# Attention scores of a two-block transformer: the heads of a unit taken in turns from both halves of the partitions

## What is computed

```
# first block, once in each of two layers: 2 key heads, each for 4 query heads
s = jnp.einsum('bnqhgd,bnkhd->bhgnqk', qb, kb)
s = jnp.where(mask, s, MASK_VALUE)
m = jnp.maximum(jnp.max(s, axis=-1, keepdims=True), sink)
p = jnp.exp(s - m)
p = p / (jnp.sum(p, axis=-1, keepdims=True) + jnp.exp(sink - m))
o = jnp.einsum('bhgnqk,bnkhd->bnqhgd', p, vb)
# second block: 8 heads, a bias of accumulated forget gates
logits = jnp.einsum('bhqd,bhkd->bhqk', qb, kh).astype(jnp.float32) * scale
logits = logits + (cqb[..., :, None] - c[..., None, :])
probs = jax.nn.softmax(logits, axis=-1)
```

## Time and profile before

| | |
|---|---|
| median of three runs | 824.11 us (824.04 to 824.52) |
| the profiled execution, its own time | 824.92 us |
| its span, first to last instruction | 823.2 us |
| TensorE matmuls | busy 808.2 us (98%) |
| weight loads | busy 730.8 us (89%) |
| VectorE | busy 597.8 us (73%) |
| ScalarE | busy 476.4 us (58%) |
| mean from memory | 182 GB/s |

### The profile page before, as it was taken

The page is one execution under the profiler, slowest core; times in us unless marked ns, Lnnn a source line. Parts: engine busy times, 40 slices in busy tenths (PEclk is TensorE's granted clock), DMA queues, the critical chain, the costliest instruction groups (busy, mean ns, idle before and its releaser), DMA issues.

```text
span 823.2 us, 12834 instructions
## 1 busy us (share of the span) xinstructions
PE 808.2 (98%) x5184; PEld 730.8 (89%) x5184; DVE 597.8 (73%) x690; ACT 476.4 (58%) x562; POOL 28.8 (3%) x63
## 2 busy tenths in 40 slices
PE   8999999999999999999999999999999999999998
PEld 8988899998998889999887999999887888888877
DVE  6799765768588787576667557556879878787793
ACT  6875775433676585543457634433368656565682
POOL 8100000000000000210000000000000000000000
PEclk9999999999999999999999999999999999999999
DMA  7545343355435633256736434455119979797921
GB/s 260 187 160 187 132 147 108 134 198 181 148 113 200 205 103 104 103 178 187 242 103 205 154 103 154 154 172 187 52 52 364 332 261 342 265 330 266 345 102 52
DMA packets 70043, 149.65 MB, mean 182 GB/s; under 512 B 8458, under 2 KB 11104, under 8 KB 69984
## 3 DMA queue, kind: packets, MB, share of 16 engines
q1 hardware_dynamic: 69568, 148.78, 52.6%
q0 software_dynamic: 384, 0.04, 0.1%
q10 hardware_dynamic: 32, 0.01, 0.0%
HBM read 147.76 MB, written 1.05 MB: 181 GB/s over the span
## 4 chain that ended last, share of the span: by engine, by line
PE 87%; DVE 8%; ACT 3%; issue 1%; DMA 1%; SPq 0%; POOL 0%; DVEq 0%; POOLq 0%; ACTq 0%
PE mm L611 11%; PE mm L613 11%; PE mm L612 11%; PE mm L595 9%; PE mm L597 9%; PE mm L596 9%; PE aux L1072 4%; PE aux L1070 4%; PE aux L1071 4%; DVE sb_w_lo L1629 3%; PE aux L703 3%; PE aux L795 3%; PE aux L736 2%; PE aux L758 1%; DVE sb_gb L1629 1%
## 5 line engine op out<-in xcount | busy, mean ns | idle before, releaser
L1629 DVE TENSOR_TENSOR sb_w_lo<-sb_raw,sb_w_hi 128x2048 fp32r<-128x2048 f32 (+2 forms) x153 | 318.7, 2095 | 58.1 <-ACT sb_w_hi L1478 26.8
L1184 ACT ACTIVATE sb_w_hi<-sb_raw 128x2048 fp32r<-128x2048 f32 (+1 forms) x83 | 155.0, 1870 | 153.9 <-PE mm L613 115.7
L611 PE MATMUL mm<-sb_hT_hi,sb_w_hi 128*128 128x256 f32 x592 | 170.0, 287 | 0.0
L613 PE MATMUL mm<-sb_hT_hi,sb_w_lo 128*128 128x256 f32 x592 | 167.4, 283 | 0.0
L612 PE MATMUL mm<-sb_hT_lo,sb_w_hi 128*128 128x256 f32 x592 | 167.4, 283 | 0.0
L1478 ACT ACTIVATE sb_w_hi<-sb_raw 128x2048 fp32r<-128x2048 f32 x50 | 95.7, 1916 | 37.2 <-PE aux L1072 18.6
L595 PE MATMUL mm<-sb_w_hi,sb_hT_hi 128*128 128x512 f32 (+1 forms) x296 | 112.1, 379 | 4.1 <-DVE sb_w_lo L1629 4.1
L611 PEld LDWEIGHTS mm<-sb_hT_hi,sb_w_hi 128*128 128x128 f32 x592 | 113.4, 192 | 1.4 <-issue 1.3
L612 PEld LDWEIGHTS mm<-sb_hT_lo,sb_w_hi 128*128 128x128 f32 x592 | 113.5, 192 | 0.0
L613 PEld LDWEIGHTS mm<-sb_hT_hi,sb_w_lo 128*128 128x128 f32 x592 | 113.4, 192 | 0.0
L597 PE MATMUL mm<-sb_w_hi,sb_hT_lo 128*128 128x512 f32 (+1 forms) x296 | 110.3, 373 | 0.0
(11 more groups left out here) (400 smaller groups left out, 1364.4 us busy)
## 6 DMA issues: line engine op xcount, KB each, us to landing
sb_raw<-in_w_in SPq DMA_DIRECT2D x120, 512.0 KB, 4.5
sb_raw<-in_w_down SPq DMA_DIRECT2D x32, 512.0 KB, 5.7
sb_raw<-in_w_gate SPq DMA_DIRECT2D x31, 512.0 KB, 4.8
sb_raw<-in_w_up SPq DMA_DIRECT2D x31, 512.0 KB, 6.2
sb_raw<-in_w_out SPq DMA_DIRECT2D x16, 512.0 KB, 4.4
sb_raw<-in_w_up_attn SPq DMA_DIRECT2D x8, 512.0 KB, 4.4
sb_raw<-in_w_up_hgrn SPq DMA_DIRECT2D x8, 512.0 KB, 4.4
sb_raw<-in_w_o SPq DMA_DIRECT2D x8, 512.0 KB, 4.4
```

Source lines behind the costliest of these rows:

```text
L611: pe.matmul(dst, w[0][:, k, cs], acts[0][:, k, :], start=start, stop=False, skip_group_check=True)
L613: return pe.matmul(dst, w[1][:, k, cs], acts[0][:, k, :], start=False, stop=stop, skip_group_check=True)
L1184: act.activation(w_hi[:, slot(t), 0:width], raw[:, slot(t), 0:width], ACT.Copy).then_inc(hi_split, 1)
L1629: return dve.tensor_tensor(out_, a, b, op)
```

## The change

`score_unit` takes the heads in turns: the j-th of the lower half of the partitions, then the j-th of the upper half. Where there is a bias, both heads' score products come first, then both biases. Units 1 and 2 now hold two heads of each half: unit 1 heads 0, 1, 4, 5 and unit 2 heads 2, 3, 6, 7. The columns of a unit are filled in the order of its list of heads, so the lower half's heads write the first bank of `aux`, the upper half's the second. Unit 0 keeps its heads and columns. VectorE's steps read and write the sinks, the gate and `a_tok` for the two heads of each half as two pieces; `pv` takes the values of the new heads. No instruction is added or taken away.

```
--- before.py
+++ after.py
@@ -90,6 +90,11 @@
 WINDOWS = [(0, 1), (0,), (1,), (1,)]
 LAST_PIECES = [(0, 0, W), (1, 0, W // 2), (1, W // 2, W)]
 OUT_PIECES = [(tt, 0, W) for tt in range(TT)] + [(tt, W + a, W + b) for tt, a, b in LAST_PIECES]
+
+
+def unit_heads(u):
+
+    return list(range(8)) if u == 0 else [4 * g + 2 * (u - 1) + i for g in range(2) for i in range(2)]
 
 
 def slot(t):
@@ -728,17 +733,20 @@
             def score_unit(turn, u, qpart, kpart, bias2):
 
                 ps = begin(turn)
-                heads = range(8) if u == 0 else range(4 * (u - 1), 4 * u)
+                heads = unit_heads(u)
+                n = len(heads) // 2
                 keys = P if u == 0 else 2 * P
-                for i, h in enumerate(heads):
-                    dst = ps[:, i * keys:(i + 1) * keys]
-                    qtt = 0 if u == 0 else 1
-                    last = pe.matmul(dst, qpart(h, qtt), kpart(h, keys), start=True, stop=not bias2)
+                qtt = 0 if u == 0 else 1
+                for j in range(n):
+
+                    for i in (j, n + j):
+                        last = pe.matmul(ps[:, i * keys:(i + 1) * keys], qpart(heads[i], qtt), kpart(heads[i], keys),
+                                         start=True, stop=not bias2)
                     if bias2:
-
-
-                        r = slice(64 * (h // 4), 64 * (h // 4) + 64)
-                        last = pe.matmul(dst, selneg[r, h * P:(h + 1) * P], cT[r, 0:keys], start=False, stop=True)
+                        for i in (j, n + j):
+                            r, h = slice(64 * (i // n), 64 * (i // n) + 64), heads[i]
+                            last = pe.matmul(ps[:, i * keys:(i + 1) * keys], selneg[r, h * P:(h + 1) * P], cT[r, 0:keys],
+                                             start=False, stop=True)
                 end(turn, last)
 
             def p_transposes(turn, u, n):
@@ -756,7 +764,7 @@
                     for i in range(4):
                         for kt in range(2):
                             last = pe.matmul(ps[:, i * 64:i * 64 + 64], pT[:, (2 * i + kt) * P:(2 * i + kt + 1) * P],
-                                             vpart(4 * (u - 1) + i, kt), start=kt == 0, stop=kt == 1)
+                                             vpart(unit_heads(u)[i], kt), start=kt == 0, stop=kt == 1)
                 end(turn, last)
 
 
@@ -1742,6 +1750,15 @@
                 m = amask[:, 2:4, :] if block2 else amask[:, 0:2, :]
                 return m.rearrange("p a b -> p (a b)").unsqueeze(1).broadcast_to([P, 4, 256])
 
+            def paired(t):
+                return t.rearrange("p (g n) -> p g n", g=2)
+
+            def heads_in(u, t):
+
+                t = paired(t)
+                n = t.shape[2] // 4
+                return t if u == 0 else t[:, :, 2 * n * (u - 1):2 * n * u]
+
             def softmax_in(u, n, turn, sinks):
 
                 nh = 8 if u == 0 else 4
@@ -1757,11 +1774,11 @@
                 release(ins, aux_free[pair], value)
                 link(dve.tensor_reduce(ast[:, 0, a:a + nh], dst, AX, ALU.max))
                 if sinks is not None:
-                    hs = sinks[:, 0:8] if u == 0 else sinks[:, 4 * (u - 1):4 * u]
-                    link(tt_(ast[:, 0, a:a + nh], ast[:, 0, a:a + nh], hs, ALU.max))
+                    hs = heads_in(u, sinks)
+                    link(tt_(paired(ast[:, 0, a:a + nh]), paired(ast[:, 0, a:a + nh]), hs, ALU.max))
                 link(ts_(ast[:, 1, a:a + nh], ast[:, 0, a:a + nh], -1.0, ALU.mult))
                 if sinks is not None:
-                    link(tt_(ast[:, 3, a:a + nh], hs, ast[:, 1, a:a + nh], ALU.add))
+                    link(tt_(paired(ast[:, 3, a:a + nh]), hs, paired(ast[:, 1, a:a + nh]), ALU.add))
                     dve.sem_inc(S["sinkexp_in"], 1)
                 dve.sem_inc(S["S_ready"], 1)
 
@@ -1769,7 +1786,6 @@
 
                 nh = 8 if u == 0 else 4
                 a = a_at(u)
-                h0 = 0 if u == 0 else 4 * (u - 1)
                 tt = 0 if u == 0 else 1
                 dve.wait_ge(S["p_ready"], n * 3 + (u + 1))
                 if sinks is not None:
@@ -1778,13 +1794,13 @@
                 link(dve.reciprocal(ast[:, 0, a:a + nh], ast[:, 2, a:a + nh]))
                 pair, value = turn
                 dve.wait_ge(aux_ready[pair], value)
-                dst = a_tok[:, tt, h0 * 64:(h0 + nh) * 64]
-                ins = tt_(dst.rearrange("p (h d) -> p h d", h=nh),
-                          aux[pair][:, 0:nh * 64].rearrange("p (h d) -> p h d", h=nh),
-                          ast[:, 0, a:a + nh].unsqueeze(2).broadcast_to([P, nh, 64]), ALU.mult)
+                dst = heads_in(u, a_tok[:, tt, :])
+                ins = tt_(dst.rearrange("p g (h d) -> p g h d", d=64),
+                          aux[pair][:, 0:nh * 64].rearrange("p (g h d) -> p g h d", g=2, d=64),
+                          paired(ast[:, 0, a:a + nh]).unsqueeze(3).broadcast_to([P, 2, nh // 2, 64]), ALU.mult)
                 release(ins, aux_free[pair], value)
                 if gate is not None:
-                    link(tt_(dst, dst, gate[:, tt, h0 * 64:(h0 + nh) * 64], ALU.mult))
+                    link(tt_(dst, dst, heads_in(u, gate[:, tt, :]), ALU.mult))
                 if u == 2:
                     dve.sem_inc(S["a_ready"], 1)
 
```

## The result

The changed kernel takes 814.70 us, median of four runs (814.28 to 815.63), against 824.32 us for the kernel before, timed again beside it (824.04 to 825.24). The ratio is 0.9883, with a 95% interval from 0.9866 to 0.9900: faster by 1.2%. The forecast was 814.6 us, its range 813.8 to 817.6. Taken again later on one chip with other kernels, the changed kernel had 814.52 us (814.23 to 815.13), ratio 0.9880 (0.9864 to 0.9897).

The account below looks back on a forecast made before the run. TensorE was taken to bound the kernel through the attentions; pairing saves 1.11 + 3.46 us in the layers and 1.44 + 3.46 in the second block, 9.47 in all, off a median of 824.11: 814.6 us, range 813.8 to 817.6.

Parts of the forecast that it names:

- What bounds the kernel: Both attention stretches: TensorE busy throughout, all nine score units on the path to the end, so time saved comes off it.
- The price of a pass, and the pairs: Score units: 0.111 us a pass at 128 keys, 0.216 at 256; every pass pairs with the other half's, saving 9.47 us.
- the old switch: Middle of the second block's S0, between heads 3 and 4: eight passes in five steps, 0.55 us instead of 0.89.
- The rest at nothing: VectorE's two writes of `a_tok` stay at 0.42 us or are covered by spare time; no new transfer, wait or instruction.
- Who is late next: P0 and weight tile 15: P0's margin falls from 2.39 to 1.5 us, the tile has 12.1; nothing subtracted.
- the sign that was named: TensorE's idle time must stay as it is; a new wait before L703 or a tile's first matmul means rival 4.
- Rival 1: Score units: the upper half's first pass starts only beside the lower's second; 7.84 us saved, 816.3 us; chance 0.06.
- Rival 2: Units of 128 keys gain nothing, as passes start no faster than 0.108 us; 6.92 us saved, 817.2 us; chance 0.06.
- Rival 3: Each change of half costs 0.2 us: 11.4 us slower, 835.5 us, chance 0.03; only the way back, 819.2 us, 0.02.
- Rivals 4 and 5: 4: TensorE waits at P0 or a weight tile, about 819.5 us, chance 0.04; 5: no effect, 824.1 us, 0.02.

Follow-up runs that it names:

- Twice the work: The changed kernel with every score unit's matmuls done twice over the same columns; 825.27 us, ratio 1.0009 to the kernel before.
- runs of two heads: The changed kernel with halves taken two heads at a time, a head's bias right behind its product; 818.43 us, ratio 0.9928 to the kernel before.
- all units side by side: The changed kernel with S1 right behind S0 in all three attentions, level product L5 moved one tile back in the layers; 813.65 us, again 813.72 us.

## Why the prediction was right

**What bounds the kernel.** Held. Twice the work in the units cost 10.6 us at the end (10.8 by the later median) for 10.5 in the units; between the first and the last unit TensorE idles 3.2 us in both kernels.

**The price of a pass, and the pairs.** Held, and it was the step with the most risk, as it took one switch in the middle of S0 for the whole. In the changed kernel every pass has its neighbour. Against the forecast lengths of 1.08, 1.06, 1.99 and 1.91 us the chain has 1.09, 1.06, 1.99 and 1.93. The sum was 9.47, the chain gives 9.54. That the time came out at 814.70 us, 0.1 us from the forecast, is partly luck: the four runs of the changed kernel lie between 814.28 and 815.63, and the profiled execution gained 0.91 us ahead of the first unit, where nothing was changed. What the prediction did not ask is why the overlap at the old switch ended at three passes. The runs of two heads show that this is a limit: with eight passes of one half in a row each change of half still saves only three or so. The new order stays clear of it, as its halves change after two passes; the prediction took the row to hold for any order.

**The rest at nothing.** Held: VectorE's two-piece writes take 0.42 us, as one piece did.

**Who is late next.** Held: 1.47 us left at P0 for a forecast of 1.5, and TensorE's idle time between the first and the last unit is the same. Outside the units the sign that was named, an idle time that stays as it is, did not hold: over the whole execution it is 16.4 us instead of 15.0. Two profiles of the changed kernel show a new wait of TensorE for VectorE, 0.9 and 1.3 us, at the small products `slot_products` of the second block's routing (L1041, far behind the attentions). It did not cost what it lasts: from the end of the last unit to the end of the span it was 332.6 us before and is 332.4 and 332.9 us in these two. And the kernel with all units side by side was profiled twice, once with this wait (1.2 us) and once without, and took 332.6 and 332.7 us for that part. Why the wait came up is open.

**Rival 1, passes keep their order of start.** Out. S1 of a layer would be 1.28 us and is 1.06. (Its price stands as 7.83 and as 7.84 us in the prediction; its terms give 7.84.) By the rule of the Trainium skill, page "TensorE: Matmul & The Clock Gate", section "Part 3: Packing small matmuls", that matmuls start and end in program order, the second block's S1 in runs of two heads would have one pair in sixteen passes, 15 steps, which is 3.4 us with the entry. It takes 2.90 us, and the trace shows the other half's first pass ahead of three passes that stand before it in the program. Here the measurement decides against the rule as far as two halves of the rows are concerned.

**Rival 2, instructions can't be fed faster.** Out: pairs of 128 keys run at 0.111 us for 16 steps on end (32 steps with twice the work), one pass in 0.056 us.

**Rival 3, a drain at every change of half.** Out: the second block's S0 changes 15 times and takes 1.99 us, 0.2 of it the entry. The change that does cost is the one between full and half height, 0.2 us each way, and putting two units side by side saved just that, 0.4 us in the chain.

**Rivals 4 and 5.** Out, by the idle time and by the result.

## What to carry to other kernels

Where products contract over 64 partitions and the operands of some lie in the lower half and of others in the upper, issue them in turns, with outputs in different banks as here: two then cost what one did, also for float32 with its two passes. Change the half after two passes if you can: runs of four lost 0.1 us a unit, and runs of eight held the other half back (2.90 us instead of 1.93 for the second block's S1). Then keep such products together, because each passage between full-height and half-height matmuls costs 0.2 us. And look first in the chain of waits whether such a switch already exists by chance in the old kernel: here the three passes saved at one switch gave the price of the whole change.

## What the runs showed of the hardware

- Loads and passes of the two halves of the rows overlap wholly: 0.111 us for a pair at 128 keys and 0.216 us at 256, the same as for one pass alone.
- A half takes in about three passes that wait beside the one that runs. This is worked out from one switch in the kernel before (16 passes in 13 steps) and from runs of eight passes, in which S0 took 23 steps of 0.111 us for 32 passes; S1, with 12.5 steps of 0.216 us for 16 passes, fits it to half a step.
- The other half's passes can start ahead of passes that stand before them in the program: in S1 in runs of eight, ahead of three.
- Passing from matmuls over 128 partitions to those over 64, or back, costs 0.2 us each, and not if both neighbours are over 128 partitions: V0 and L6 have no such extra. Where two units stand side by side, with the wait for a buffer between them, it is gone.
- Runs of exactly four passes lose 0.1 us in a unit that comes back to the lower half, once and not at every change, at 128 keys (1.19 against 1.09 us) as at 256 (2.03 against 1.93 us); the reason was not looked for.
- Writing two banks in turns from one half saves nothing (1.92 us as before).
